# A hybrid decoder step on one core: 24 instead of 16 sample tokens gathered one by one, gate maps spread over chunks 80 to 121, and edits to two attention stages

## What is computed

```python
def one_block(xb):                      # xb: normed tokens
    q = (xb @ w_pq).reshape(TOKEN_BLOCK, PEER_HEADS, PEER_DKEY)
    s1 = jnp.einsum('thd,kd->thk', q[..., :half], sub_k1)
    s2 = jnp.einsum('thd,kd->thk', q[..., half:], sub_k2)
    v1, i1 = lax.top_k(s1, PEER_TOPK)
    v2, i2 = lax.top_k(s2, PEER_TOPK)
    ...
    best, pos = lax.top_k(cand, PEER_TOPK)
    eidx = jnp.take_along_axis(cidx, pos, axis=-1)
    gate = jax.nn.softmax(best.astype(jnp.float32), axis=-1)
    u = expert_u[eidx]
    act = jax.nn.gelu(jnp.einsum('td,thkd->thk', xb, u).astype(jnp.float32), approximate=False)
    vv = expert_v[eidx]
    return jnp.einsum('thk,thkd->td', (gate * act).astype(xb.dtype), vv)
```

## Time and profile before

| | us |
|---|---|
| three runs | 2305.84, 2310.10, 2310.73 (median 2310.1) |
| the profiled execution | 2311.11 |
| its span | 2309.2 |
| mean granted TensorE clock | 0.984 of full speed |
| VectorE, ScalarE, GpSimd busy | 1179, 301, 386 |
| moved by DMA | 843 MB, 365 GB/s over the span |

### The profile page before, as it was taken

How to read it: one execution, slowest core, us unless ns; L and a number is a source line. 1 busy time by engine, 2 the same in 40 slices (tenths; PEclk the granted TensorE clock), 3 DMA queues, 4 the chain that set the end, 5 groups by cost and what they waited for, 6 DMA issues and landing times.

```text
span 2309.2 us, 35404 instructions
## 1 busy us (share of the span) xinstructions
PE 2207.9 (96%) x14282; PEld 2015.7 (87%) x14282; DVE 1179.1 (51%) x2095; ACT 301.2 (13%) x926; POOL 386.3 (17%) x414
## 2 busy tenths in 40 slices
PE   7999998789889879999999999999999999999998
PEld 5677776577589868999999999899999999999998
DVE  3200003833566647767777544599744444444422
ACT  2000001722221012011111110144200000000000
POOL 0100000022302011232212221133311111111100
PEclk9999999999999989999999999999999999999999
DMA  7999982289959898999999999999999999999974
GB/s 280 405 413 381 385 316 81 80 333 357 398 201 396 345 383 315 407 398 422 422 421 420 420 420 420 372 372 376 402 422 421 422 422 421 422 422 422 421 315 155
DMA packets 117787, 843.21 MB, mean 365 GB/s; under 512 B 14432, under 2 KB 16608, under 8 KB 30656
## 3 DMA queue, kind: packets, MB, share of 16 engines
q1 hardware_dynamic: 62752, 485.30, 52.4%
q0 software_dynamic: 54128, 354.58, 37.7%
q10 hardware_dynamic: 816, 2.11, 0.2%
HBM read 834.25 MB, written 74.78 MB: 394 GB/s over the span
## 4 chain that ended last, share of the span: by engine, by line
PE 64%; DMA 23%; DVE 8%; issue 2%; ACT 1%; POOL 1%; SPq 0%; DVEq 0%; POOLq 0%; ACTq 0%
PE low L1414 39%; PE big L1414 24%; DMA BIG<-expert_u,VB 20%; DVE BIG L1240 4%; DMA WR<-wall 1%; DMA BIG<-kaT 1%; ACT BIG L630 1%; DMA BIG<-expert_v,VB 1%; DMA BIG<-memT 0%; DMA BIG<-va 0%; DVE CST L968 0%; POOL BIG L525 0%; DVE BIG L846 0%; PE low L1538 0%; DVE HT L883 0%
## 5 line engine op out<-in xcount | busy, mean ns | idle before, releaser
L1414 PE MATMUL low<-HT,WR 128*128 128x176 f32 (+3 forms) x6336 | 1081.9, 333 | 8.4 <-DMA WR<-wall 7.0
L1414 PEld LDWEIGHTS low<-HT,WR 128*128 128x128 f32 x6336 | 984.2, 191 | 98.2 <-issue 9.7
L1414 PE MATMUL big<-BIG,WR 128*128 (+3 forms) x2888 | 450.7, 312 | 11.3 <-DVE XT L891 7.1
L1253 DVE SCALAR_TENSOR_TENSOR XT<-BIG,VB,XT 128x2048 f32<-128x2048 f32 x128 | 300.9, 2351 | 302.7 <-DMA BIG<-expert_v,VB 302.4
L1414 PE MATMUL low<-BIG,WR 128*128 (+3 forms) x2616 | 434.8, 321 | 12.6 <-DMA WR<-wall 10.3
L1414 PEld LDWEIGHTS big<-BIG,WR 128*128 128x128 f32 x2888 | 419.3, 193 | 30.1 <-issue 18.5
L1240 DVE SCALAR_TENSOR_TENSOR BIG<-BIG 128x2048 f32<-128x2048 f32 x144 | 329.5, 2291 | 210.8 <-DMA BIG<-expert_u,VB 209.7
L1414 PEld LDWEIGHTS low<-BIG,WR 128*128 128x128 f32 x2616 | 411.0, 192 | 17.8 <-issue 10.5
L539 POOL DMA_INDIRECT BIG<-expert_u,VB x144 | 161.5, 1122 | 683.8 <-DVE BIG L1240 609.5
L545 POOL DMA_INDIRECT BIG<-expert_v,VB x144 | 161.5, 1122 | 558.2 <-DVE XT L1253 477.3
L914 DVE TENSOR_SCALAR BIG<-low 128x320 f32 x32 | 15.7, 492 | 264.0 <-PE low L1414 264.0
(11 more groups left out here) (230 smaller groups left out, 1124.0 us busy)
## 6 DMA issues: line engine op xcount, KB each, us to landing
WR<-uT SPq DMA_DIRECT2D x128, 1024.0 KB
WR<-expert_v SPq DMA_DIRECT2D x128, 1024.0 KB
WR<-wall SPq DMA_DIRECT2D x122, 1024.0 KB
BIG<-va POOLq DMA_DIRECT2D x48, 512.0 KB, 11.0
BIG<-kaT POOLq DMA_DIRECT2D x64, 384.0 KB, 11.0
BIG<-kmT SPq DMA_DIRECT2D x2, 2048.0 KB, 12.9
BIG<-vm SPq DMA_DIRECT2D x8, 512.0 KB, 13.4
XT<-xT SPq DMA_DIRECT2D x1, 2560.0 KB, 21.9
```

What stands on the lines that cost most here:

```text
L1253: nc.vector.scalar_tensor_tensor(out=x_tok, in0=rows_of(row), scalar=weight, in1=x_tok, op0=ALU.mult, op1=ALU.add).then_inc(s_vsum, 1)
L1414: return nc.tensor.matmul(out, lhsT, rhs, start=start, stop=stop, skip_group_check=True)
```

## The change

Sizes and plan of the stage of experts:

```diff
-FEW = 16
+FEW, FEWER = 16, 8
+ALONE = FEW + FEWER
 REST = NT - P
-DENSE = REST - FEW
+DENSE = REST - ALONE
-EXPS, TAIL = 64, 80
-TURN = 92
-MAP_LO, MAP_HI = 100, 124
+EXPS, TAIL = 56, 64
+TURN = 72
+MAP_LO, MAP_HI = 80, 122
+E2_AT = 98
-ROWS = SLOTS + FEW
+ROWS = SLOTS + FEW + FEWER
+ROOM = 22528
+V_FEW = (*range(SLOTS, SLOTS + FEW), *range(40), *range(SLOTS + FEW, ROWS), *range(40, SLOTS))
+FEWER_AT = V_FEW.index(SLOTS + FEW)
 ROWS_AHEAD = 50
-ROWS_BEFORE = 141
+ROWS_WEIGH = 98
+ROWS_BEFORE = 108
...
-    return 2 if c % 3 == 0 else 1
+    return 2 if c % 4 == 0 else 1
...
-FEW_OUT = 96
+FEW_OUT, FEWER_OUT = 32, 96
```

```diff
+                for half in range(2):
+                    to, k = half * 64 + h * FEWER, h * PK + half * FEWER
+                    act.dma_start(chosen[to:to + FEWER, :, SLOTS + FEW:ROWS], fewer_src[:, :, k:k + FEWER]).then_inc(s_few, 16)
...
+                if row[0] == SLOTS:
+                    dve.wait_ge(s_udot, SLOTS)
+                    nc.vector.tensor_copy(h_tok.rearrange(...), HT_by[:, :, P + FEW:P + ALONE]...).then_inc(s_rep, 1)
...
-                if n % 3 == 0 and later:
+                if (n - ROWS_AHEAD) % 5 in (0, 2) and later:
                     choose_part(*later.pop(0))
...
-                if n == ROWS_AHEAD + 3 * 3 * (len(GROUPS) - OF_FIRST) + 2:
+                if n == ROWS_WEIGH:
...
-            dve.wait_ge(s_few, 16 * PH)
+            dve.wait_ge(s_few, 16 * 3 * PH)
...
-                if g >= 4:
-                    pe.wait_ge(s_gcp, g - 3)
+                if g >= 3:
+                    pe.wait_ge(s_gcp, g - 2)
...
-                    mm(bank[4 + g % 4][:, j * P:(j + 1) * P], hot[1][g % 2][:, j], hot[0][g % 2][:, j]).then_inc(s_gm, 1)
+                    mm(bank[4 + g % 3][:, j * P:(j + 1) * P], hot[1][g % 2][:, j], hot[0][g % 2][:, j]).then_inc(s_gm, 1)
...
+            pe.wait_ge(s_vsum, FEWER_AT + FEWER)
+            for k in range(KT):
+                mm(v_all[k][:, FEW:ALONE], h_few[:, k * P:(k + 1) * P], pick_fewer, start=False, stop=True)
```

Prompt attention gets a third buffer for probabilities in the place of queries that are no longer needed, from pair 5 on, and the negated maximum goes to ScalarE ahead of the division of the pair before, all of which comes behind it:

```diff
+def pair_in_buffer(p):
+    if p < OF_THREE:
+        return p - 2
+    return -1 if p == OF_THREE else p - 3
...
-                    if p >= 2:
-                        dve.wait_ge(s_T, 2 * p - 2)
+                    if pair_in_buffer(p) >= 0:
+                        dve.wait_ge(s_T, 2 * pair_in_buffer(p) + 2)
...
-                if last:
-                    dve.wait_ge(s_dv, mr)
-                    nc.vector.tensor_scalar(pl[:, 0, 0:256], ...)
-                    nc.vector.tensor_scalar(pl[:, 0, 256:384], ...).then_inc(s_nrm, 1)
                 if now:
                     dve.wait_ge(s_dv, m4)
...
                 if last:
-                    nc.vector.tensor_scalar(pl[:, 1, 0:256], ...)
-                    nc.vector.tensor_scalar(pl[:, 1, 256:384], ...).then_inc(s_nrm, 1)
+                    dve.wait_ge(s_dv, mr)
+                    nc.vector.tensor_scalar(wide_l[:, 0], ...)
+                    nc.vector.tensor_scalar(narrow_l[:, 0], ...).then_inc(s_nrm, 1)
+                    nc.vector.tensor_scalar(wide_l[:, 1], ...)
+                    nc.vector.tensor_scalar(narrow_l[:, 1], ...).then_inc(s_nrm, 1)
```

In sample attention VectorE does some work of the first tile ahead of the next request's softmax instead of behind it, co tiles from 6 on use three banks, and the loads of memory keys and values move in SyncE's order (km and vm of the first four requests three chunks later; two of the four value loads of the second group directly behind them, into other room):

```diff
-                if n + 1 < REQ:
-                    softmax_s(n + 1)
-                for f in (*with_scores, *with_turn):
+                for f in with_scores:
                     add_to_stream(FIRST_TILE, CROSS, f)
...
+                if n == 4:
+                    keep_cross_query(FIRST_TILE, 1)
+                    keep_cross_query(FIRST_TILE, 2)
+                if n + 1 < REQ:
+                    softmax_s(n + 1)
+                for f in with_turn:
+                    add_to_stream(FIRST_TILE, CROSS, f)
...
-                at = f % 2 if stage == "pq" else 5 + f % 2
+                at = f % 2 if stage == "pq" else (5, 6, 0)[(f - 6) % 3] if stage == "co" and f >= 6 else 5 + f % 2
...
-                if before == POS["out", 1, 15]:
+                if before == POS["cq", 1, 0]:
                     sp.wait_ge(s_used, FREED["out", 1, 15])
                     mem_keys(0)
-                    mem_values(0)
+                    mem_values(0, 0, 4)
+                    sp.wait_ge(s_sc, 3)
+                    sp.wait_ge(s_idx, 3)
+                    mem_values(1, 0, 2)
...
                     sp.wait_ge(s_cV, 1)
-                    mem_values(1)
+                    mem_values(1, 2, 4)
```

More of the change, by code:

```diff
@@ L223, in build @@
         VTF = QK[:, T_VA * NT:T_IN * NT]
-        probs_p = VTF[:, 0:1536].rearrange("p (b s c) -> p b s c", b=2, s=2)
+        probs_two = VTF[:, 0:1536].rearrange("p (b s c) -> p b s c", b=2, s=2)
+        q_pairs = [QK[:, (T_QA + 2 * i) * NT:(T_QA + 2 * i + 2) * NT].rearrange("p (s t) -> p s t", s=2) for i in range(2)]
         probsT_p = VTF[:, 1536:2304].rearrange("p (s c) -> p s c", s=2)
@@ L293, in build, with probs_p @@
         x_tok = XT_by[:, :, 0:P]
+        def probs_p(p):
+            buffer = p % 2 if p < OF_THREE else (2, 1, 0)[(p - OF_THREE) % 3]
+            if buffer == 2:
+                return q_pairs[0][:, :, 0:256], q_pairs[1][:, :, 0:P]
+            return probs_two[:, buffer, :, 0:256], probs_two[:, buffer, :, 256:384]
         def rows_of(x):
@@ L1339, in _ @@
             dve.wait_ge(s_turn, 1)
-            dve.wait_ge(s_few, 16 * PH)
-            own = P - FEW
+            dve.wait_ge(s_few, 16 * 3 * PH)
+            own = P - ALONE
             for z in range(3):
-                nc.vector.tensor_copy(turned[z][:, 0:own], bank[6][:, z * P + FEW:(z + 1) * P])
+                nc.vector.tensor_copy(turned[z][:, 0:own], bank[6][:, z * P + ALONE:(z + 1) * P])
                 nc.vector.tensor_copy(turned[z][0:64, own:DENSE], bank[7][0:64, z * 64:(z + 1) * 64])
@@ L1695, in values_c @@
                         for n in range(4):
-                            ins = mm(bank[5][32 * n:32 * n + 32, :], pT[:, b * P + 32 * n:b * P + 32 * n + 32], vm[n][:, b * 512:(b + 1) * 512], start=(b == 0), stop=(b == 1))
+                            ins = mm(bank[5][32 * n:32 * n + 32, :], pT[:, b * P + 32 * n:b * P + 32 * n + 32], vm[r][n][:, b * 512:(b + 1) * 512], start=(b == 0), stop=(b == 1))
                     ins.then_inc(s_cV, 1)
@@ L1882, in gate_maps, with turn_fewer @@
                     pe.wait_ge(s_turnev, 1)
-                if g >= 4:
-                    pe.wait_ge(s_gcp, g - 3)
+                if g >= 3:
+                    pe.wait_ge(s_gcp, g - 2)
                 for j in range(4):
                     pe.wait_ge(s_weighed, 4 * g + j + 1)
-                    mm(bank[4 + g % 4][:, j * P:(j + 1) * P], hot[1][g % 2][:, j], hot[0][g % 2][:, j]).then_inc(s_gm, 1)
+                    mm(bank[4 + g % 3][:, j * P:(j + 1) * P], hot[1][g % 2][:, j], hot[0][g % 2][:, j]).then_inc(s_gm, 1)
+            def turn_fewer(part):
+                pe.wait_ge(s_rep, 2)
+                if part:
+                    pe.wait_ge(s_fewer_h, part)
+                for k in range(4):
+                    at = (4 * part + k) * P
+                    ins = nc.tensor.transpose(bank[7][:, k * P:(k + 1) * P], h_tok[:, at:at + P], ident)
+                ins.then_inc(s_fewer_t, 1)
             done = 0
@@ L1906, in dense_v @@
                         pe.wait_ge(s_dev, NCH - UB + k // 2 + 1)
-                    ins = mm(v_all[k][:, FEW:REST], WR[:, slot_of(r) * D + k * P:slot_of(r) * D + (k + 1) * P], coefs, start=(first and k % 2 == 0), stop=last)
+                    ins = mm(v_all[k][:, ALONE:REST], WR[:, slot_of(r) * D + k * P:slot_of(r) * D + (k + 1) * P], coefs, start=(first and k % 2 == 0), stop=last)
                     if last:
```

106 lines of the change are left out of this document (65 added, 41 removed).

## The result

The changed kernel takes **2323.4 us** (2317.7 to 2328.1, four runs) against 2310.1 for the kernel before: ratio 1.0061, interval 1.0035 to 1.0086. It is slower by 0.6%. The forecast was 2303 us, range 2287 to 2323, and slower had a chance of 0.20: it missed in sign, and the time lies just outside the range. The profiled execution took 2322.4 us, its span is 2320.6 (forecast 2302.1).

A forecast was written before the change was run, and what follows sets the result against it. TensorE and the gathered-row queue, sharing full DMA bandwidth, were taken as bounds, with rows finishing last. From a span of 2309.2 us, plus 11.4 for experts, minus 18.5 ahead of them, came 2302.1; forecast 2303 us, range 2287 to 2323.

The forecast's parts named there:

- two runners and a shared track: Expert stages: row queue and TensorE share full DMA bandwidth, half each in V, giving a chunk every 4.97 us.
- The stop: U stage after row 107: VectorE waits for turned choices and map 0, so the row queue idles some 60 us.
- Stage end 2320.6, 11.4 later than before: End of the expert stages in the clock of before: rows finish last, 11.4 us later in total.
- I take 5.58: Gate maps in U: each chunk with a map takes 5.58 us, limited by the track, with 1.25 rows.
- The restart: U rows resuming after their idle time: the sum starts them with map 0, at 1380 us, without extra time.
- Tail, 17.6: After the last V row: remaining additions and the norm take 17.6 us, from 20 less 2.4.
- The front, 18.5: Attention, co tiles and memory loads ahead of U: edits there save 18.5 us (6 to 30).
- Last rows at 4.93: End of V: the last 11.6 rows keep 4.93 us each, costing 25 us more, 2328 us; chance 0.12.
- Front swallowed: Ahead of U: a full track takes back gains, leaving some 9 us saved, 2312 us; chance 0.15.
- TensorE ahead at the stop: U stage: map 0 comes at 1369 us, rows restart 11 us earlier, total 2292 us; chance 0.17.
- Weight-load floor: Expert chunks: weight loads set a minimum instruction spacing, 6 to 7 us later, 2309 us; chance 0.04.
- TensorE sets the end: V stage: DMA does not hold it, so TensorE's 54 us are saved in full, 2238 us; chance 0.02.

The follow-up runs named there:

- changed_again: The changed kernel unaltered, measured again beside other runs on the same chip: ratio 1.0047 to the kernel before.
- experts_alone: The changed kernel with its edits to prompt attention, sample attention, co tiles and memory loads taken back, expert edits kept: 2335.5 us, ratio 1.0107.
- spread_turnings: The changed kernel with the four turnings of repeated tokens at chunks 97, 100, 103 and 106 instead of 98 to 101: ratio 1.0054.
- balanced: The changed kernel with VectorE leaving rows after row 119, not 107, turnings at chunks 88, 91, 94, 97, and fewer rows behind chunk 122: 2287.6 us.
- front_alone: The kernel before with only the edits of prompt attention, sample attention, co tiles and memory loads: 2293.1 us, ratio 0.9919.
- rows_120: The changed kernel with VectorE leaving its rows after row 119 instead of 107 and the turnings at chunks 92 to 95: 2295.8 us, ratio 0.9931.

## Why the prediction was wrong

**What held.** The model of two runners and a shared track held: the earlier trace rows's 4.97 us came back as V's pace (2044.61 and 2049.58 are two starts on the same half of PSUM, one chunk apart, below), a 168-column instruction takes 0.143 us (forecast 0.142), and row 107 starts at 314.5 us from U's start (forecast 315.6). The stop was where the forecast put it and nearly as long: no rows for 69 us (forecast 65), and TensorE goes on behind map 0 at 1368.45 - 984.38 = 384.1 from U's start (forecast 383). The rate in it was 269 GB/s, not 230. The row queue became the last runner; rows alone on the track followed each other every 2.8 us (twelve starts from 2267.35 to 2297.76), and the V stage from first row to last took 724 us, as summed.

```profile
2044.61 2.54 PE L1466 MATMUL big<-BIG,WR 128*128 x16
...
2049.58 2.54 PE L1466 MATMUL big<-BIG,WR 128*128 x16
```

**The step that failed** is the stage sum of the experts, "Stage end 2320.6, 11.4 later than before". It is 24.0 later in the changed kernel's trace (1336.2 - 1312.2), 26.0 and 26.5 in changed_again and experts_alone, so 13 to 15 us were missing. The largest missing piece is the term of the maps, "I take 5.58". Term by term, in the changed kernel:

- *Maps.* From row 108 to row 151 the forecast had 34 chunks of 5.58, 190 us; it was 196.6, and 200.6 in changed_again. The forecast let both queues slow down together: 5.58 us a chunk for TensorE and, at 1.25 rows a chunk, 4.46 a row. In the trace TensorE does not slow down but for the turnings and the stop at them: between its maps lie 5.45 us (1367.56 to 1460.27 are 17 chunks), and it waits for no weight chunk. The rows alone pay. From 1390 to 1478, nearly all of it ahead of the stop, the track moved 420 GB/s, as full as the forecast had it: 16.98 MB of the stream (queue 1, below) in 88 us, a chunk each 5.4, and 19.86 MB of rows (queue 0), a row each 4.6. In spread_turnings it was a row each 4.5 (38.10 MB from 1385 to 1550). The first fence shows maps in PE's timeline, the last of them that of row 151's chunk; the second is the DMA in the window 1390 to 1478, with packets, MB and share.

```profile
1367.56 1.05 PE L1466 MATMUL big<-HT 128*128 128x128 f32 x8
...
1460.27 1.05 PE L1466 MATMUL big<-HT 128*128 128x128 f32 x8
...
1560.37 1.05 PE L1466 MATMUL big<-HT 128*128 128x128 f32 x8
```
```profile
q0 software_dynamic: 2725, 19.86, 54.6%
q1 hardware_dynamic: 2333, 16.98, 46.4%
```

This could be worked out before, as an estimate: a chunk each 5.45 us takes 1.0486/5.45 = 0.192 of the 0.421 MB/us, and from the other 0.229 a row comes each 1.0486/0.229 = 4.58 us, 43 x 4.58 = 197. It fits 196.6 and the 196.3 of spread_turnings, but it leaves out the restart, for which three rows stood ready, and no run varied the split by itself. Over the whole stretch the mean rate is only 404 GB/s, because it is 343 in the first 20 us, while the row queue starts again, and 371 from 1478 to 1503, behind TensorE's stop. The lower rate of the map stage of before would have been no guide either. There, from 1500 to 1650, TensorE is busy all but without a gap, and VectorE waits for row loads for only 6.2 us between 1485 and 1659: 377 GB/s is what the two asked for, not what the track could give. The first of three windows:

```profile
1500.00:1550.00 50.00, 50.00 (x365) 50.00 (x365) 44.50 (x62) 20.68 (x81) 16.44 (x12) 1.00 0.91 371
```

- *The restart.* Row 108 does not start with map 0 but 1.9 us behind it, after one-hots and the application of the map; from the 383 of the sum it is 3.0 us.
- *Tail, 17.6.* It took 2320.6 - 2300.1 = 20.5, 2.9 more. TensorE had idled for 29.6 us and began the last sum at the lower of its clocks (0.50, windows at the end):

```profile
2302.87 7.34 PE L1466 MATMUL big<-BIG,CST 128*128 128x192 f32 x32 [29.64 <-DVE XT L1449]
```


The same 32 instructions took 5.44 in balanced, behind a wait of 1.95: 1.9 of the 2.9 us. The other 1.0 stays open.

- *The front, 18.5.* By itself it is 18.7. The size of each part was about right, that of the memory loads by luck. In this profiled execution the front was worth 12.6 (996.95 - 984.38), in the twelve traces with it 12.6 to 18.8 against the one trace of before. That is scatter of a term that one trace can't give better than by a few microseconds, and the forecast had it from 6 to 30.

6.6 + 3.0 + 2.9 + 5.9 = 18.4, and the span was missed by 18.5. All four have the same sign.

**The rivals.** *Last rows at 4.93*: out, by those twelve starts. *Front swallowed*: out by front_alone and its parts (this rival's 9 us against 18.7). *TensorE ahead at the stop*: map 0 was where the main forecast had it, not 11 us earlier. *Weight-load floor*: the trace speaks against it, 0.143 us at 168 columns against the 0.150 at 176 of the earlier trace rows, the whole gain of 6.6 ns that was summed; at this width the rule of the Trainium skill (TensorE: Matmul & The Clock Gate, Back-to-back issue gap) sets no floor that can be seen. *TensorE sets the end*: out.

**The weighing.** The slower side of the forecast rested on one mishap, the last rows. It held no case in which the forecast's own mechanism was right and each size came out a little worse, though the stop (60 us of an idle queue) was in the text as "the weak place". Its own bounds, 2294 to 2313, covered the unknown prices of added operations and not the pace of the rows beside a TensorE that takes all it wants.

## What to carry to other kernels

When two queues share a full track, count the loads that are *not* issued while one queue is stopped: 72 us at 269 GB/s were ten loads, and moving twelve loads ahead of the stop was worth 27 to 30 us. Sum each queue by itself. In the maps the chunk stream asked for less than half of the track (a chunk each 5.45 us) and got it, and the rows had the rest, 4.6 us each; in V, where the stream could use more than half, both had 4.97. A low rate in a window says nothing of the track as long as neither queue is waited for. Plan the stage so that both runners end together. Stops of the engine that isn't last are worth little: spreading the turnings gained nothing while the rows ended 25 us behind TensorE. Between rows_120 and balanced, 8.5 us apart, the turnings and the rows behind chunk 122 changed together, so what each earned there is not shown.

## What was not expected of the hardware

- In the V stage the row queue beside the stream and the stream beside the row queue had some 4.97 us each in every kernel of the study (422 GB/s from 1750 to 2150 us, 418 in rows_120). In the maps the split was not even: 193 GB/s for the stream, 226 for the rows.
- TensorE's clock fell behind waits of a few microseconds in an otherwise full stream, to 0.50, the lower of its two levels (1.2 of 2.4 GHz), and came back within 4 to 6 us (behind the wait at 1591 it reads 0.56 from 1595 to 1597 and 1.00 from there). Three windows of the changed kernel, behind waits of 3.6, 29.6 and (the same, later) 29.6 us, then one of balanced, behind a wait of 1.95 us, where it stayed at 1.00:

```profile
1591.40:1595.00 3.60, 3.57 (x15) 3.60 (x16) 2.95 (x4) 1.11 (x6) 0.10 (x1) 0.50 1.00 416
2302.80:2306.50 3.70, 3.63 (x11) 3.66 (x12) 3.66 (x8) 3.70 (x15) 0.00 (x0) 0.50 0.00 0
2306.50:2310.30 3.80, 3.71 (x22) 3.42 (x21) 0.30 (x1) 0.07 (x2) 0.00 (x0) 0.97 0.67 276
```
```profile
2267.20:2272.70 5.50, 5.44 (x32) 5.14 (x32) 3.89 (x8) 3.68 (x16) 0.00 (x0) 1.00 0.15 63
```
- Twelve traces of kernels with the same front have U start between 978.1 and 984.4 us: 6 us of scatter, ahead of a stage that repeats within 2 (changed and changed_again). Where it comes from is not shown.
